# Hybrid decoder step on one core: RMS scale applied at the eviction of gate and up, squares summed per column group, expert outputs added to y by DMA, one unused indirect fetch ahead

## What is computed

```
# layer 0, after sparse attention
hp = hp + attention(...) @ w_o
xn = rms_norm(x, g);  x = x + (silu(xn @ w_gate) * (xn @ w_up)) @ w_down      # D_FF = 2816
...
# layer 1, after the S5 state space
top_v, top_i = top_k(xn @ w_router + b_router, 2)
combine = one_hot(top_i) weighted by softmax(top_v)
for e in range(8):
    h = silu(xn @ w_gate[e]) * (xn @ w_up[e])
    out = out + combine[:, e:e+1] * (h @ w_down[e])                            # D_FF_EXPERT = 2816
x = x + out
```

## Time and profile before

| | us |
|---|---|
| timed runs, median (lowest to highest) | 1647.05 (1642.23 to 1649.59) |
| profiled execution, its own time | 1642.71 |
| its span in the trace | 1641.1 |
| PE busy in the span | 1447.5 |
| DVE busy | 1193.7 |
| ACT busy | 879.8 |
| POOL busy | 225.9 |

### The profile page before, as it was taken

The page is one execution under the profiler, slowest core; times in us unless marked ns, Lnnn a source line. Parts: engine busy times, 40 slices in busy tenths (PEclk is TensorE's granted clock), DMA queues, the critical chain, the costliest instruction groups (busy, mean ns, idle before and its releaser), DMA issues.

```text
span 1641.1 us, 27646 instructions
## 1 busy us (share of the span) xinstructions
PE 1447.5 (88%) x10403; PEld 1297.8 (79%) x10403; DVE 1193.7 (73%) x1859; ACT 879.8 (54%) x1580; POOL 225.9 (14%) x211
## 2 busy tenths in 40 slices
PE   6997978989998876359779999999999999999994
PEld 4784547879998775238678999999999999999993
DVE  3076553575453688994469999999999999999995
ACT  2322342424343321014467878778787777878872
POOL 3034000790000055360000000000000000000001
PEclk9998798999999955559889999999999999999997
DMA  9246624334445200005348999999999999999982
GB/s 349 80 142 183 219 93 158 116 116 154 155 170 192 88 2 1 1 1 200 144 149 342 355 375 358 375 362 361 377 350 375 356 372 364 354 380 353 373 325 101
DMA packets 52172, 382.35 MB, mean 233 GB/s; under 512 B 6658, under 2 KB 11842, under 8 KB 24002
## 3 DMA queue, kind: packets, MB, share of 16 engines
q1 hardware_dynamic: 46594, 366.71, 59.8%
q0 software_dynamic: 2848, 8.65, 1.6%
q10 hardware_dynamic: 2592, 5.15, 0.8%
HBM read 372.98 MB, written 7.51 MB: 232 GB/s over the span
## 4 chain that ended last, share of the span: by engine, by line
PE 78%; DVE 11%; issue 4%; ACT 3%; POOL 2%; DMA 2%; SPq 0%; ACTq 0%; DVEq 0%; POOLq 0%
PE ps L948 10%; PE ps L950 10%; PE ps L949 10%; PE ps L967 5%; PE ps L487 5%; PE ps L969 5%; PE ps L968 5%; PE ps L489 4%; PE ps L488 4%; PE ps L475 4%; POOL arena L2108 2%; DVE ring_lo L1424 2%; PE ps L805 2%; PE ps L807 1%; PE ps L806 1%
## 5 line engine op out<-in xcount | busy, mean ns | idle before, releaser
L948 PE MATMUL ps<-split 128*128 128x256 f32 x1408 | 405.0, 288 | 4.7 <-DVE split L1941 2.6
L950 PE MATMUL ps<-split 128*128 128x256 f32 x1408 | 399.6, 284 | 0.0
L1956 DVE TENSOR_TENSOR ring_lo<-ring,split 128x2048 fp32r<-128x2048 f32 x132 | 302.4, 2291 | 42.7 <-ACT split L1323 42.7
L949 PE MATMUL ps<-ring_lo,split 128*128 128x256 f32 x1056 | 299.7, 284 | 0.0
L948 PEld LDWEIGHTS ps<-split 128*128 128x128 f32 x1408 | 269.2, 191 | 15.4 <-DVE split L1941 3.0
L950 PEld LDWEIGHTS ps<-split 128*128 128x128 f32 x1408 | 269.1, 191 | 0.0
L1323 ACT CAST split<-ring 128x1024 fp32r<-128x1024 f32 x264 | 264.8, 1059 | 0.0
L1424 DVE TENSOR_TENSOR ring_lo<-ring,chunk_hi 128x1024 fp32r<-128x1024 f32 x100 | 144.3, 1445 | 164.4 <-ACT chunk_hi L1029 163.9
L1029 ACT CAST chunk_hi<-ring 128x1024 fp32r<-128x1024 f32 x100 | 104.7, 1048 | 210.6 <-PE ps L489 163.8
L949 PEld LDWEIGHTS ps<-ring_lo,split 128*128 128x128 f32 x1056 | 202.3, 192 | 3.2
L489 PE MATMUL ps<-xn_lo,chunk_hi 128*128 128x288 f32 x608 | 182.6, 300 | 0.0
(11 more groups left out here) (333 smaller groups left out, 2824.6 us busy)
## 6 DMA issues: line engine op xcount, KB each, us to landing
ring<-wmoe SPq DMA_DIRECT2D x132, 1536.0 KB, 8.7
arena<-wmoe SPq DMA_DIRECT2D x44, 1536.0 KB, 8.9
ring<-wpre SPq DMA_DIRECT2D x41, 1536.0 KB, 6.7
ring<-ckv SPq DMA_DIRECT2D x32, 256.0 KB, 3.0
arena<-ckv SPq DMA_DIRECT2D x32, 256.0 KB, 2.9
yrow<-arena ACTq DMA_DIRECT2D x8, 512.0 KB, 10.2
arena<-cki SPq DMA_DIRECT2D x32, 64.0 KB, 2.0
arena<-cki POOLq DMA_DIRECT2D x32, 64.0 KB, 5.5
```

The source lines that it names most:

```text
L948: mm(o, xg_hi[:, buf, k, :], wg_hi[:, c.i % 2, w], start=(k == 0), stop=False)
L949: mm(o, xg_hi[:, buf, k, :], lo[:, w], start=False, stop=False)
L950: m = mm(o, xg_lo[:, buf, k, :], wg_hi[:, c.i % 2, w], start=False, stop=(k == KD - 1))
L1956: V.tensor_tensor(moe_slot_lo(slot)[:, w], moe_slot(slot)[:, w], wg_hi[:, c.i % 2, :], ALU.subtract).then_inc(S["mw_lo"], 1)
```

## The change

Four things. (1) The second norm's scale 1/rms is no longer multiplied into x before the split; the split takes x times gain, and DVE multiplies gate and up by 1/rms when they leave PSUM. The squares of a column group are taken by ACT and summed by PE one group at a time, behind the w_o groups. (2) An expert's sum is multiplied by the gate weight as it leaves PSUM, and POOL adds its rows to y in DRAM by an indirect DMA with add; y is preset with x by three stores of SP. The six fetches, `yrow` and `add_rows` go. (3) POOL makes one indirect fetch into an unused place ahead of the experts. (4) The chunk numbers of select, find and gather move, `weights_of` is cut short and moves to chunk 1.

```diff
-J_SELECT, J_FIND, J_GATHER = 2, 4, 12
+J_WEIGHT, J_SELECT, J_FIND, J_GATHER = 3, 6, 8, 14
 # PE
+        def square_sum(k):
+            pe.wait_ge(S["sq"], k + 2)
+            m = mm(ps[:, 7, 0:T], ones, xsq[:, k % 2, :], start=(k == 0), stop=(k == KD - 1))
+            m.then_inc(S["ss"], 1)
         for mch in range(8):
             n, part = U_WO + mch // 3, mch % 3
...
+            project_split(ps[:, mch % 4, 0:T], mch, 0 if mch == 0 else None, wo_hi, wo_lo).then_inc(S["wo_mm"], 1)
...
+            if mch:
+                square_sum(mch - 1)
+        square_sum(KD - 1)
-        norm_sums(1)
...
+            if ck == J_WEIGHT:
+                first_weight()
 # ACT
+        def residual_high(k, i, done):
+            act.wait_ge(S[done], k + 1)
+            a(xn_hi_at[:, k, :], x[:, k, :], ACT.Copy, scale=gains[i][:, k:k + 1]).then_inc(S["xn_hi"], 1)
+            if k >= 2:
+                act.wait_ge(S["ss"], k)
+            a(xsq[:, k % 2, :], x[:, k, :], ACT.Square).then_inc(S["sq"], 1)
         for c in range(2, C_GU + 2):
             chunk_high(c)
+            if c >= 3 and c - 3 < KD - 1:
+                residual_high(c - 3, 1, "wo")
+        residual_high(KD - 1, 1, "wo")
-        norm(1)
-        input_high(xn_hi_at, 1)
...
-            a(sg[:, f % 2, :], ps[:, f % 3, 0:T], ACT.Silu).then_inc(S["gsil"], 1)
+            act.wait_ge(S["gn"], f + 1)
+            a(sg[:, f % 2, :], sg[:, f % 2, :], ACT.Silu).then_inc(S["gsil"], 1)
...
-        def expert_sum(n, rows):
+        def expert_sum(n, buf):
             act.wait_ge(S["unit"], n * NF + (U_PRE + NF))
             act.wait_ge(S["yout"], n * 16)
-            cp(yn, ps[:, 3:5, :].rearrange("p a b -> p (a b)")).then_inc(S["my"], 1)
-            act.wait_ge(S["my"], n + 1)
-            act.dma_start(rows, yn).then_inc(S["yout"], 16)
+            a(yn, ps[:, 3:5, :].rearrange("p a b -> p (a b)"), ACT.Copy, scale=gsl[:, buf:buf + 1]).then_inc(S["my"], 1)
 # DVE
+        def gate_scaled(f):
+            if f == 0:
+                dve.wait_ge(S["rt"], 2)
+                link(V.reciprocal(rstd, rstd))
+            dve.wait_ge(S["gu_mm"], 2 * f + 1)
+            if f >= 2:
+                dve.wait_ge(S["h"], f - 1)
+            V.tensor_tensor(sg[:, f % 2, :], ps[:, f % 3, 0:T], rstd, ALU.mult).then_inc(S["gn"], 1)
+            dve.wait_ge(S["gu_mm"], 2 * f + 2)
+            link(V.tensor_tensor(hT[:, f, :], ps[:, 3 + f % 3, 0:T], rstd, ALU.mult))
         def h_chunk(f):
             dve.wait_ge(S["gsil"], f + 1)
-            dve.wait_ge(S["gu_mm"], 2 * f + 2)
-            V.tensor_tensor(hT[:, f, :], sg[:, f % 2, :], ps[:, 3 + f % 3, 0:T], ALU.mult).then_inc(S["h"], 1)
+            V.tensor_tensor(hT[:, f, :], hT[:, f, :], sg[:, f % 2, :], ALU.mult).then_inc(S["h"], 1)
...
+        def index(n, buf, added):
             dve.wait_ge(S["find_mm"], n + 1)
+            dve.wait_ge(S["yout"], added * 16)
...
-            if ck == J_FIND + 2:
+            if ck == 1:
                 weights_of()
 # POOL
+        turn_link(g.memset(slot_tok[:, :], 0))
+        pool.indirect_dma_start(v(M_RT + N_RT, NPARAM), None, dr["params"],
+                                bass.IndirectOffsetOnAxis(ap=slot_tok[:, 0:1], axis=0)).then_inc(S["kidx"], 16)
+        pool.wait_ge(S["kidx"], 16 * (NB // 2 * NPG + 1))
...
+        def add_rows(n):
+            buf = n % 2 if n < NE else 0
+            pool.wait_ge(S["my"], n + 1)
+            pool.indirect_dma_start(dr["y"], bass.IndirectOffsetOnAxis(ap=slot_out[:, buf:buf + 1], axis=0),
+                                    yn, None, compute_op=ALU.add).then_inc(S["yout"], 16)
+        gather(0)
+        pool.wait_ge(S["out"], 16 * 3)
         for n in range(NE):
-            gather(n)
+            if n < NE - 1:
+                gather(n + 1)
+            add_rows(n)
-        pool.wait_ge(S["yout"], 16 * NE)
-        rows_of(0)
```

More of the change, by code:

```diff
@@ L447, in _ @@
                         expert_load(j % MSLOTS, e * NF + j)
[L448 to L452, removed]
+            sp.wait_ge(S["yout"], 16 * NE * ROUNDS)
+        sp.wait_ge(S["yout"], 16 * NE)
         sp.wait_ge(S["out"], 16 * 3)
@@ L476, in project, with project_split @@
             return m
-        def project_split(out, c, run=None, hi=xn_hi_at):
+        def project_split(out, c, run=None, hi=xn_hi_at, low=xn_lo_at):
             n, part, _, _ = split_chunk(c)
@@ L488, in project_split @@
                 mm(out, lo[:, w], hi[:, k, :], start=False, stop=False)
-                m = mm(out, chunk_hi[:, c % 2, w], xn_lo_at[:, k, :], start=False, stop=(k == KD - 1))
+                m = mm(out, chunk_hi[:, c % 2, w], low[:, k, :], start=False, stop=(k == KD - 1))
             return m
@@ L920, in find, with first_weight @@
             for i, (t0, nt) in enumerate(BLK):
[L921 removed]
+                m = mm(ps[:, 7, 0:3], onehot[0:nt, i, :], tr[0:nt, i, :], start=(i == 0), stop=(i == 2))
             m.then_inc(S["find_mm"], 1)
+        def first_weight():
+            pe.wait_ge(S["wgt"], 1)
+            for i, (t0, nt) in enumerate(BLK):
+                m = mm(ps[:, 7, 2:3], onehot[0:nt, i, :], tr[0:nt, i, 2:3], start=(i == 0), stop=(i == 2))
+            m.then_inc(S["wgt"], 1)
         def turn_rows(n):
@@ L1425, in chunk_low, with input_low, residual_low @@
                             ).then_inc(S["chunk_lo"], 1)
-        def input_low(run, hi):
+        def input_low(run, hi, lo):
             for k in range(KD):
-                low(run, k, hi)
+                dve.wait_ge(S["xn_hi"], KD * run + k + 1)
+                V.tensor_tensor(lo[:, k, :], xn[:, k, :], hi[:, k, :], ALU.subtract).then_inc(S["xn_lo"], 1)
+        def residual_low(run, k, i):
+            dve.wait_ge(S["xn_hi"], KD * run + k + 1)
+            V.scalar_tensor_tensor(out=xn_lo_at[:, k, :], in0=x[:, k, :], scalar=gains[i][:, k:k + 1],
+                                   in1=xn_hi_at[:, k, :], op0=ALU.mult, op1=ALU.subtract).then_inc(S["xn_lo"], 1)
         dve.wait_ge(S["const"], 80)
@@ L2010, in _ @@
                 m = V.tensor_copy(selr[:, :, w], selm)
+                V.tensor_copy(wgtr[:, :, w], comb)
             link(m)
-            link(V.tensor_scalar(row, row, float(-CAP), None, ALU.add))
-            for rd in range(2, ROUNDS):
-                link(V.tensor_scalar(prod, pos, float(CAP * rd), float((NE - 1) * CAP), ALU.is_ge, ALU.mult))
-                link(V.tensor_tensor(row, row, prod, ALU.add))
-            link(V.scalar_tensor_tensor(out=kept, in0=pos, scalar=float(CAP), in1=selm, op0=ALU.is_ge, op1=ALU.mult))
-            ranks(1)
-            posc, selc = v(M_RT + 240, 24 * (ROUNDS - 1)), v(M_RT + 320, 24 * (ROUNDS - 1))
+            posc, selc, wgtc = (v(M_RT + o, 24 * (ROUNDS - 1)) for o in (240, 320, 400))
             with dve.Fori(0, (ROUNDS - 1) * NE) as m:
                 column = lambda a: lambda nt, i: a[0:nt, bass.ds(m + 8 * (ROUNDS - 1) * i, 1)]
-                select(m + NE, column(posc), column(selc))
-                index(m + NE, 0)
+                select(m + NE, column(posc), column(selc), column(wgtc))
+                index(m + NE, 0, m + NE)
                 gathered_all(m + NE, 0)
@@ L2173, in shape_constants @@
     put("rsel", (p[:, None] // 16) % 2 == np.arange(2)[None, :])
-    put("tok", np.stack([t0 + p for t0, _ in BLK], 1))
+    put("tok", np.stack([t0 + p for t0, _ in BLK] + [T + p], 1))
     cb = np.zeros((P, NCONSTB), np.float32)
```

135 lines of the change are left out of this document (57 added, 78 removed).

## The result

The changed kernel takes 1688.62 us (median of four runs, 1687.81 to 1692.61), the kernel before 1645.28 beside it: a ratio of 1.0266, 95% interval 1.0236 to 1.0297. The forecast was slower, 1667 us, in a range of 1650 to 1685. The direction was right; the size was about half, and the time lies 3.6 us above the range.

The account below looks back on a forecast made before the run. PE was taken to set the pace, any wait in its order being paid in full. Terms -1.8 + 1.4 + 3 - 2.7 - 1.5 + 26 + 11 - 13 = +22.4 us led to 1667 us, range 1650 to 1685.

Parts of the forecast that it names:

- Squares per column group: Second norm behind the w_o groups: gain of 15.6 us less 13.8 for six steps with PE waits of 1.9, net -1.8.
- The upper bound of 5: Second norm: most the clock could cost at the waits between w_o groups, three falls of 1.6 us.
- 1/rms at eviction: Gate and up stage: +1.4 us in the first hidden chunk, +3 for DVE's added products beside POOL's tables.
- Experts' start: Ahead of the first expert: unused fetch speeds the first gather, presets of y partly beside it; -2.7 us (-3.8 to +1).
- First-use cost: POOL's first gather issues in 4.75 us, the second 0.96; the unused fetch could take up to 3.8 off.
- Borders and clock: Seven expert borders: PE waits 3.7 us each on DVE's split, +26 us; lower TensorE clock behind them, +11.
- The first rival: Weight stream sets the pace, loads run ahead during border stops and PE catches up: 1632 us, 4%.
- The second: Clock holds at the expert borders and the last add is quick: +8, 1651 to 1655 us, 12%.
- Gate weights: Experts: short weights_of removes three PE waits, -2.4 us; three small f32 matmuls add +0.9; net -1.5.
- The end: End of program: one indirect add, 7.5 us with hand-over, replaces 20.5 us; gain of 13 (10 to 16).
- Slow adds beside the weight stream: Rival in the expert stage: late adds stop DVE, and PE behind it, six times; at 36 us +60, 1727, 4%.
- the deciding 26: Expert stage: us from an add's issue, about chunk 2, to the index at chunk 8; later landing stops DVE.

Follow-up runs that it names:

- c1: The changed kernel run once more with no edit: 1687.52 us, ratio 1.0251 to the kernel before.
- e1: Changed kernel with ACT's scaled copy and square of a column group ahead of the cast that waits for the next group: 1662.91 us, ratio 1.0108.
- e7: Changed kernel with ACT's square of a column group ahead of the scaled copy, the cast staying ahead of both: 1672.05 us, ratio 1.0166.
- e4: Changed kernel with Silu writing gate back into PSUM, so DVE's product reads one operand from there: 1677.83 us, ratio 1.0192.
- e3: Changed kernel with DVE's two subtractions for expert 0 moved away from the first gather: 1680.46 us, ratio 1.0219.
- e6: Kernel before, without the change or a fetch ahead, with DVE's two subtractions moved away from the first gather: 1638.61 us, ratio 0.998.
- e2: Changed kernel with J_GATHER back from 14 to 12, so the next expert's last split ends at chunk 19: 1642.49 us, ratio 0.9996.
- e5: Changed kernel with the next expert's last column group split ahead of ACT's last cast and DVE's subtraction, J_GATHER still 14: 1659.71 us, ratio 1.0088.
- e9: Changed kernel with POOL's eight indirect transfers writing their rows into y instead of adding them: one run, 1683.04 us.

## Why the forecast was half the size, step by step

**Squares per column group: the step that failed.** Its waits were right, 1.96 against 1.9. What failed is the sentence "A stretch of 2.8 without a matmul was followed by a clock of 1.00, so I add nothing for the clock at 1.9". One stop that kept the clock was taken as a bound for all shorter ones. Four of the six stops of 1.96 were followed by 0.50, and each cost 1.5 us (7.43 to 5.91). The upper bound of 5 ("three falls of 1.6") was too small as well. The seventh stop brought the clock down too, and the last stretch to the first gate chunk took 8.1 instead of 6.3. A second, smaller error is the f32 sum: halving a row read at 0.50 gave 0.4, and it takes 0.75. So even the steps that kept the clock took 5.9 where I had 5.5. These are 6.1 + 1.8 + 2.5, 10.4 in all. The step was forecast at -1.8 and measured +7.6 in that profile and +6.7 in c1 (of the 10.4, 1 us falls out, since the six steps of before had taken 20.1 and not 6 x 3.19). e1 shows the cause: without the waits, the clock stays. e7 shows that 0.4 us of stop less is enough.

**1/rms at eviction.** Forecast +4.4, measured +5.2: the size fits, the composition does not. I had said that the product's new form costs nothing more, since its row beside POOL was as fast as any. That row had one operand in PSUM; it said nothing about the form with two in SBUF. By e4 the form costs 3.6 us, and all else in this stretch 1.6 (158.0 against 156.4). The first hidden chunk, forecast at +1.4, has 5.05 us between two casts of ACT (306.39 to 311.44) where before had 3.19, so +1.9; for the two added products, forecast at +3, nothing is left. The Trainium skill ("SBUF — State Buffer", "Who interferes with whom"), which I had cited and set aside, has it that a VectorE instruction with two SBUF inputs contends with a GpSimd instruction that reads SBUF and one with a single SBUF input does not. The trace agrees: 1.90 against 0.45 us, and the two products out of PSUM (L1711, L1713) stay at 0.45 in the same stretch. The prediction's number by this rule, 3.6 us, came out by luck: it took three products at 1.65, paid in full, and there were five at 1.90, of whose 7.3 us half was paid.

**Experts' start.** Forecast -2.7, measured +1.1; the mechanism was wrong. "First-use cost" was read from one slow and one quick row without asking what lay beside the slow one. e3 and e6 show that it was DVE's subtractions. The +1.1 lies in the down projection, 75.2 us from its first to its last row against 73.9. I had no term for it. PE's list of waits in that stretch has a row that before lacks:

```profile
PE ps L810 <- DVE ring_lo L1443: 1.2, 1, 1.2
```

PE waits once for DVE's subtraction of a down chunk; why DVE comes late there no run took apart.

**Borders and clock.** Forecast 26 + 11, measured 24.4 + 14.1 by e2. The stop was read right to 0.2 us from a place where nobody waited. The clock fell at all seven, and its price lay inside the bounds of 0 to 17. The first rival (the stream repays the stops) is refuted by e2, where all of it came back. The second (the clock holds) is refuted for stops of 3.5 us; e5 shows that it would have been right for 1.56.

**Gate weights.** Forecast -1.5; the experts of e2, without stops, take 2.3 us less than before. PE's list shows no wait near the place of the earlier trace rows any more.

**The end.** Forecast -13, measured -10.7. ACT's scaled copy ends 9.1 us ahead of the end (9.8 in c1) where I had 7.5. The landing was right: the last add is the shortest of the eight, 6.5 against my 7. Between it and the end of the program lie 2.3 us, and those I left out. The Trainium skill's sentence ("DMA: Bandwidth & Descriptors", "Rules for kernel authors") that an accumulating transfer reads its destination and writes it later gave -11 through twice the fetch. e9 doesn't bear out a doubling: the add takes 1 to 2.6 us more than a write. So that number came out right for another reason.

**Slow adds beside the weight stream.** They land after 13.4 us, above my upper row of 10.2 but below the deciding 26, and no wait on them shows. That rival is out.

Some 5 us remain that no part of the change explains. They go with the granted clock in the stretch ahead of it (c1), move single profiles and may be in the medians as well: of the eight timed runs of the changed kernel one took 1680.23 us and the others over 1687. Whether the change has a part in that is not shown.

## What to carry to other kernels

A stop of the bound engine is not only its own length: behind a stop of 3.5 us the clock's price added more than half again (14.1 to 24.4), so look for the split, cast or copy that can be put ahead of the row that it waits behind. One number in a schedule was worth 38 us here, one exchanged pair of rows 10, and neither changes the work. Before a slow first instance is called a first-use cost, look at what the other engines do in the same microseconds; and a row that shows an instruction unharmed beside another engine bounds only that form of it, operands' places included.

## What was not expected of the hardware

- The clock behind short stops is not ordered by their length alone: none of 13 stops of 1.5 us (six of e7, seven of e5) cost it, four of six of 1.96 did, in each of the seven profiles with this stage unedited, three of six of 2.3 did, and seven of seven of 3.5. A stop of 2.8 in the earlier trace rows kept it. Behind equal stops of 3.5 the clock stayed at 0.50 for 3.3 to 6.0 us. The places differ too: 4 to 5.5 us of work lie between two stops of the w_o groups and about 98 between two borders of e5, and no run has the same stop in both.
- An indirect DMA's issue on POOL stretches from 1.03 to 4.80 us beside two subtractions of DVE with both operands in SBUF. The Trainium skill ("SBUF — State Buffer", "Who interferes with whom") infers that such a two-input operation does not hold up GpSimd's making of descriptors. Here it held up the issue by 3.8 us, and the measurement decides; whether it is the descriptors or POOL's reading of the row numbers that waits, no run separates.
- The same product of 128x288 takes 0.46 us alone and up to 3.11 beside POOL, while one that reads an operand from PSUM keeps its 0.45.
